# A transformer kernel with two blocks: fetched expert rows moved to a later stage, and the first projections and two stage seams put in another order

## What is computed

```
xn = rmsnorm(h, norm1_w); proj = xn @ w_in            # first block
h = h + (g_d * (o_d @ w_branch_diff) + g_c * (o_c @ w_branch_chunk)) @ w_out
h = h + peer(rmsnorm(h, norm2_w), ...)                # experts
h = rmsnorm(h, final_norm_w)
h = concat(meta, h)                                   # second block, 528 tokens
for layer in (0, 1):                                  # 0: gated deltanet, 1: mLSTM
    h = h + mixer(rms_norm(h, attn_norm[layer]))
    f = relu(rms_norm(h, ffn_norm[layer]) @ ff_up)
    h = h + (f * f) @ ff_down
```

## Time and profile before

| | us |
|---|---|
| median of 3 runs | 3837.25 |
| lowest, highest | 3832.71, 3839.84 |
| the profiled execution, its own time | 3834.99 |
| its span in the trace | 3833.2 |
| PE busy in the span | 3612.8 (94%) |
| DVE busy | 2439.8 (64%) |
| ACT busy | 1604.8 (42%) |
| POOL busy | 726.8 (19%) |

### The profile page before, as it was taken

One profiled execution on the slowest core, in us unless ns is written; L12 is line 12 of the kernel. 1 busy time (PEld: TensorE's weight loads), 2 busy tenths in 40 slices (PEclk: granted clock), 3 DMA queues, 4 the chain that ended last, 5 costly groups with the idle time before them and its releaser, 6 DMA issues.

```text
span 3833.2 us, 60211 instructions
## 1 busy us (share of the span) xinstructions
PE 3612.8 (94%) x24325; PEld 3370.2 (88%) x24325; DVE 2439.8 (64%) x4877; ACT 1604.8 (42%) x3002; POOL 726.8 (19%) x618
## 2 busy tenths in 40 slices
PE   7999999999999999999899999999899999979999
PEld 5777878999898999999788888888799989979999
DVE  5665349997768888888676676666643433455242
ACT  4555324336863333333454444443432335454141
POOL 0000004775443333332121111110000011010000
PEclk9999999999999999999899999999999999989999
DMA  3122224777889898989253332221222212212221
GB/s 122 61 67 69 91 83 138 239 240 245 257 293 338 318 345 319 331 318 338 71 82 55 61 63 57 60 61 31 73 88 94 94 34 67 67 56 83 94 94 61
DMA packets 208149, 542.30 MB, mean 141 GB/s; under 512 B 18665, under 2 KB 92905, under 8 KB 207873
## 3 DMA queue, kind: packets, MB, share of 16 engines
q1 hardware_dynamic: 99792, 341.22, 26.3%
q0 software_dynamic: 42048, 150.49, 13.7%
q10 hardware_dynamic: 66032, 46.75, 3.9%
HBM read 492.14 MB, written 46.25 MB: 140 GB/s over the span
## 4 chain that ended last, share of the span: by engine, by line
PE 65%; DVE 13%; ACT 12%; issue 5%; DMA 4%; ACTq 1%; POOL 1%; PEldq 0%; DVEq 0%; PEld 0%; POOLq 0%
PE bank L106 64%; ACT wh L127 4%; DVE wl L133 3%; DMA raw<-in_v 2%; ACT gb L127 2%; DVE acc L143 2%; ACT oh L127 1%; DVE row L179 1%; ACTq L187 1%; PE bank L109 1%; ACT L121 1%; DVE aal L133 1%; ACT rt L127 1%; DVE fs L133 1%; ACT L127 1%
## 5 line engine op out<-in xcount | busy, mean ns | idle before, releaser
L106 PE MATMUL bank<-Xh,wh 128*128 128x256 f32 (+3 forms) x3680 | 1222.4, 332 | 41.6 <-DVE Xl L133 21.0
L106 PE MATMUL bank<-Xl,wh 128*128 128x256 f32 (+3 forms) x3680 | 1156.8, 314 | 0.0
L106 PE MATMUL bank<-Xh,wl 128*128 128x256 f32 (+3 forms) x3680 | 1156.0, 314 | 0.0
L127 ACT ACTIVATE wh<-raw 128x1024 fp32r<-128x1024 f32 (+1 forms) x632 | 587.8, 954 | 678.0 <-PE bank L106 560.4
L133 DVE TENSOR_TENSOR wl<-raw,wh 128x1024 fp32r<-128x1024 f32 (+1 forms) x539 | 573.6, 1083 | 428.9 <-ACT wh L127 423.5
L106 PEld LDWEIGHTS bank<-Xh,wh 128*128 128x128 f32 x3680 | 705.6, 192 | 109.8 <-issue 65.6
L106 PEld LDWEIGHTS bank<-Xh,wl 128*128 128x128 f32 x3680 | 703.9, 191 | 20.6
L106 PEld LDWEIGHTS bank<-Xl,wh 128*128 128x128 f32 x3680 | 706.4, 192 | 17.6 <-issue 0.3
L133 DVE TENSOR_TENSOR H<-H,bank 128x256 f32<-128x256 f32 (+3 forms) x394 | 183.9, 469 | 325.8 <-PE bank L106 324.0
L106 PE MATMUL bank<-aah,wh 128*128 128x384 f32 x1024 | 350.9, 343 | 17.3 <-DVE wl L133 12.1
L106 PE MATMUL bank<-aal,wh 128*128 128x384 f32 x1024 | 347.9, 340 | 0.0
(11 more groups left out here) (340 smaller groups left out, 5940.0 us busy)
## 6 DMA issues: line engine op xcount, KB each, us to landing
raw<-in_u SPq DMA_DIRECT2D x128, 512.0 KB
raw<-in_v SPq DMA_DIRECT2D x128, 512.0 KB
raw<-in_up SPq DMA_DIRECT2D x64, 512.0 KB, 3.9
raw<-in_down SPq DMA_DIRECT2D x64, 512.0 KB, 3.3
scratch<-gb ACTq DMA_DIRECT2D x12, 2048.0 KB, 12.6
gj<-scratch SPq DMA_DIRECT2D x32, 768.0 KB
raw<-in_w_gdn SPq DMA_DIRECT2D x48, 512.0 KB
raw<-in_w_att SPq DMA_DIRECT2D x36, 512.0 KB
```

The source lines that it names most:

```text
L106: return Issued(self, self.q and self.q.matmul(out, l, r, start=start, stop=stop), 1)
L127: return Issued(self, self.q.activation(out, in_, func, **kw), 1)
```

## The change

ROWS_FIRST goes from 56 to 32, so that no row step lies beside the one-hots and 224 are left for the second part, with other numbers in some(n) and ONEHOT at 1.9. The first three projections take x times the norm weight, split on ACT and DVE into ODH and ODL (buffers that attention fills later), without the inverse root; DVE multiplies that in as it evicts (first_copy); each projection is a group of its own, and the norm blocks, which later projections read, lie between. DVE's first wait is for cols alone. Ahead of each feed-forward stage the last two sums of squares go behind the first two of the first three groups, and the norm of the second half behind the first three groups' relu2. The core of the diff (of the two raw_x the first is DVE's, the second ACT's; constants is DVE's):

```diff
-ONEHOT = 2.3
+ONEHOT = 1.9
-ROWS_FIRST = 56
+ROWS_FIRST = 32
 ...
         def first_unit():
+            x1 = [(16, 528)]
+            sums_begin("norm1", x1, PA)
+            for k in range(8):
+                if k < ADDED:
+                    sums_part("norm1", 16, k, f"x_in{k // 2}", 0)
+                do("raw_x", k)
+                if k == 3:
+                    prepare(1)
+            prepare(1)
+            def project(kind):
+                n = slab("w_att", kind)
+                (QT, KT, VT)[kind].take(0)
+                g = ATT_G[0, kind] = group(PD, by_slab(n), of(ODH, ODL), 512, lambda k: (("rxl", k),))
+                dense_now(g)
+                return n, g
+            def evict(kind, n, g):
+                do("first_copy", kind)
+                given_back(g, "qkv0", 0, kind)
+                done_with(n, g)
+            first = project(0)
+            for k in range(ADDED, 8):
+                sums_part("norm1", 16, k, f"x_in{k // 2}", 0)
+            prepare(1)
+            sums_end("norm1", x1)
+            second = project(1)
+            evict(0, *first)
+            for k in range(4):
+                norm_block("norm1", 16, 528, k)
+            third = project(2)
+            evict(1, *second)
+            for k in range(4, 6):
+                norm_block("norm1", 16, 528, k)
+            VF.take(0)
+            evict(2, *third)
+            for k in range(6, 8):
+                norm_block("norm1", 16, 528, k)
+            do("constants_in")
+            do("lam")
 ...
-                merge((itertools.chain(back(m, 1, 4), back(m + 1, 0, 0)), 32), (weighted(d), 44), (some(4), 4))
+                merge((itertools.chain(back(m, 1, 4), back(m + 1, 0, 0)), 32), (weighted(d), 44), (some(5), 5))
 ...
-                    side = some(6 + n % 2)
+                    side = some(8)
                     for j in (2 * (n % 2), 2 * (n % 2) + 1):
                         neurons(g, (j,))
                         next(side, None)
-                    merge((steps, 16), (side, 4 + n % 2))
+                    merge((steps, 16), (side, 6))
 ...
-        def ffn(layer):
+        def ffn(layer, behind):
-            sums_end(f"ffn{layer}", halves[1:])
-            xf = normed(f"ffn{layer}", halves, done=(halves[0][0],))
+            def xf(a, k):
+                return (("xl", f"ffn{layer}", a, k),)
 ...
-                        dense_together(gs)
+                        first = (half, fbs[0], a) == (0, 0, halves[0][0])
+                        if first:
+                            dense_together(gs[:2])
+                            for x in behind:
+                                sums_part(*x)
+                            sums_end(f"ffn{layer}", halves[1:])
+                            dense_now(gs[2])
+                        else:
+                            dense_together(gs)
 ...
+                        if first:
+                            for k in range(8):
+                                norm_block(f"ffn{layer}", *halves[1], k)
 ...
             def constants():
-                dv.wait_ge("const", 2)
-                dv.wait_ge("ones", 1)
+                dv.wait_ge("cols", 0)
+            def raw_x(k):
+                dv.wait_ge("rxh", k)
+                dv.stt(ODL[:, k, :], H[:, k, 16:528], col("norm1", k), ODH[:, k, :].bitcast(F32), ALU.mult,
+                       ALU.subtract).then_inc("rxl", k)
+            def first_copy(kind):
+                g = ATT_G[0, kind]
+                b = clear(dv, (QT, KT, VF)[kind], 0)
+                dv.wait_ge("rinv", "norm1", 16)
+                dv.wait_ge("dense", g)
+                dv.tt(b, PS[PD.at["g", g]], RT.at["norm1", 16][:, 0:512], ALU.mult).then_inc("qkv0", 0, kind)
 ...
+            def raw_x(k):
+                if k == 0:
+                    ac.wait_ge("cols", 0)
+                if k >= ADDED:
+                    ac.wait_ge(f"x_in{k // 2}", 0)
+                ac.act(ODH[:, k, :], H[:, k, 16:528], ACT.Copy, scale=col("norm1", k)).then_inc("rxh", k)
```

More of the change, by code:

```diff
@@ L607, in build, with xn @@
         do("lam_load")
[L608 to L615, removed]
+        def xn(a, k):
+            return (("xl", "norm1", a, k),)
         QT = Ring([alloc("qt", 512) for _ in range(2)])
@@ L631, in first_unit @@
         def first_unit():
[L632 to L635, removed]
-            VF.take(0)
[L637 to L642, removed]
+            x1 = [(16, 528)]
[30 more added lines that the diff above has]
+                norm_block("norm1", 16, 528, k)
+            VF.take(0)
+            evict(2, *third)
[3 more added lines that the diff above has]
+            do("lam")
         def proj_att(u):
@@ L1320, in last_outputs @@
                         prepare(1)
-            for x in behind:
-                sums_part(key, *x)
             for s in ws:
                 done_with(s, g)
+            return [(key, *x) for x in behind]
         GW = []
@@ L1708, in build @@
         ROOM[0] = room_at, more_room(("up0", "down0"), 1, 3, (("so", 7, 8), ("vnm", 7, 8), ("sn", 7, 7, 1)), room_at)
-        last_outputs(0, [("gdn_out", 14), ("gdn_out", 15)], OX.at[7], "ogl", XQ7, last_outs())
-        ffn(0)
+        behind = last_outputs(0, [("gdn_out", 14), ("gdn_out", 15)], OX.at[7], "ogl", XQ7, last_outs())
+        ffn(0, behind)
         fence()
@@ L1963, in build @@
         ROOM[1] = room_at, more_room(("up1", "down1"), 1, 3, (("mo", 3, 8), ("msn", 3, 7), ("mnum", 3, 2)), room_at)
-        last_outputs(1, [("ml_out", 6), ("ml_out", 7)], OX1.at[3], "mogl", XQ3, last_third())
-        ffn(1)
+        behind = last_outputs(1, [("ml_out", 6), ("ml_out", 7)], OX1.at[3], "mogl", XQ3, last_third())
+        ffn(1, behind)
         do("store")
@@ L1998, in constants, with constants_in @@
             def constants():
-                pe.wait_ge("const", 2)
                 pe.wait_ge("ones", 1)
+            def constants_in():
+                pe.wait_ge("const", 1)
             def dense(g, k):
@@ L2323, in pe_program @@
             program(pe, dict(
-                fence=fence, constants=constants, dense=dense, rms_sum=rms_sum, rms_total=rms_total, rms_part=rms_part, meta_sum=meta_sum, att_vt=att_vt, scores=scores, transp=transp,
+                fence=fence, constants=constants, constants_in=constants_in, dense=dense, rms_sum=rms_sum, rms_total=rms_total, rms_part=rms_part, meta_sum=meta_sum, att_vt=att_vt, scores=scores, transp=transp,
                 values=values, key_scores=key_scores, first_scores=first_scores, weights_out=weights_out, x_rows=x_rows, row_sums=row_sums,
@@ L2913, in dv_program @@
             program(dv, dict(
-                fence=fence, constants=constants, split=split, norm=norm, rms_part=rms_part, meta_reduce=meta_reduce, meta_scale=meta_scale, meta_low=meta_low, both_inv=both_inv, resid=resid, lam=lam, scores=scores,
+                fence=fence, constants=constants, constants_in=constants_in, raw_x=raw_x, first_copy=first_copy, split=split, norm=norm, rms_part=rms_part, meta_reduce=meta_reduce, meta_scale=meta_scale, meta_low=meta_low, both_inv=both_inv, resid=resid, lam=lam, scores=scores,
                 weigh=weigh, att_split=att_split, gated=gated, merge=merge, top16=top16, first_top=first_top, pairs=pairs, picked=picked,
@@ L2933, in constants @@
             def constants():
-                ac.dma(CB_, X["cols"][:, :]).then_inc("const", 0)
-                ac.dma(ROWP[0:16, 0:4], X["rows"][:, :]).then_inc("const", 1)
-                ac.dma(CST, X["cst"].rearrange("p (a b) -> p a b", a=9)).then_inc("const", 2)
+                ac.dma(CB_, X["cols"][:, :]).then_inc("cols", 0)
+                ac.dma(ROWP[0:16, 0:4], X["rows"][:, :]).then_inc("const", 0)
+                ac.dma(CST, X["cst"].rearrange("p (a b) -> p a b", a=9)).then_inc("const", 1)
                 ac.dma(H[:, :, 0:16], X["meta"].rearrange("p (k t) -> p k t", k=8)).then_inc("meta", 0)
@@ L3377, in ac_program @@
             program(ac, dict(
[L3378 removed]
+                fence=fence, constants=constants, split=split, rms_sum=rms_sum, rms_squares=rms_squares, rms_part=rms_part, rms_inv=rms_inv, norm=norm, raw_x=raw_x, x_load=x_load, meta_square=meta_square, meta_inv=meta_inv, meta_high=meta_high, both_inv=both_inv, lam=lam, att_copy=att_copy,
                 att_vt=att_vt, exps=exps, transp=transp, att_out=att_out, att_split=att_split, gate=gate,
```

9 lines of the change are left out of this document (5 added, 4 removed).

## The result

| | before | after |
|---|---|---|
| median of 5 runs, us | 3838.46 | 3858.34 |
| lowest, highest | 3832.71, 3839.84 | 3856.56, 3861.34 |
| span of the profiled execution | 3833.2 | 3855.8 |

The account below looks back on a forecast made before the run. PE, busy 94%, was taken as the bound, so only its waits could give time back. Terms -4 - 7 - 4 + 7 - 2.5 = -10.5 put the profiled execution near 3824.5 us, the median near 3827; range 3811 to 3845.

Parts of the forecast that it names:

- Start: Start of the kernel: first scores reach DVE at 47.8 instead of 52.74; -4 us, bounds 0 and -12.8.
- Seams: Both feed-forward seams: PE's waits shorten and the second half ends earlier; -3.5 us each, -7 together, bounds 0 and -13.3.
- two of the three first groups end near 2739.1, inside today's wait: First seam: these groups run while PE now waits 6.93 us for the last squares.
- What is late next is this second norm: Seams: the second half's norm, behind three relu2, replaces the squares as the late part; a wait of 3 to 4 us.
- One-hots: One-hot stage and choice of experts: -18.5 us, held spills seven to four, against +14.3 in the choice; -4 net.
- Second part: Weighted and neuron rounds: 24 more row steps and gathers cost +7 us in all, bounds 0 and +37.
- I let a third of it through: Neuron rounds: six steps add 7.5 us of DVE each; a third of that reaches the time, +7 in all.
- hidden by 4 us of slack: Weighted rounds: one more row step adds 1.25 us to DVE's 30.5 of 34.5, at no cost.
- slower: Rival, 0.12: DVE's in-order list bounds the second part, from some 95% share in neuron stretches; 30 instead of 7, 3850 us.
- Last round: Last round of the second part: without row steps DVE no longer delays the transpositions; -2.5 us, bounds 0 and -4.
- Transfers: Rival, 0.09: DMA at 356 GB/s bounds the neuron rounds; three pay 21 us instead of 7, 3841.
- the 358 GB/s: Rule against the forecast: HBM bound per core, neuron rounds not under 74.6 us, some 20 us added instead of 7.

Follow-up runs that it names:

- e4_rows_flat: The kernel after with its additional row steps in the weighted rounds alone (10 each; 26 in a neuron round, 6 in the last): 3846.15 us, 1.0026.
- e8_filled: The kernel after with the same row steps, one standing between DVE's af and the next slab's low part in neuron rounds: 3836.78 us, 0.9995.

## Why the prediction was wrong

- **Start** (-4): the mechanism and its times came out, within 1 us for most. The row quoted for the slow clock has 3.75 us for four matmuls, so it doesn't give the 0.43 of the working, but in after the first projection's matmuls do stand 0.43 apart. The end of the kernel doesn't show the gain (between -2.3 and +4.6); the sum took it as kept to the end.
- **Seams** (-7): they cost 4.6 where they stand, and 2.9 of that came back between them. The failed step is "two of the three first groups end near 2739.1, inside today's wait". I asked only when their input is ready. The groups need three banks, which the last three additions to H hold; the matmuls then ran at a clock of 0.51, close to 1.2 GHz, and the sums came behind them. "What is late next is this second norm" was right, and worth 4.9 a seam.
- **One-hots** (-4 net): -22.4 and +14.1, so -8. The price in the choice and the count of held spills were right; the holds also got shorter, which I had not allowed for.
- **Second part** (+7): +27.7. The failed step is "I let a third of it through". All of it went through in the neuron rounds, 1.2 us a step (20.9 for the 18 that `e4_rows_flat` took out), and 0.2 a step in the weighted ones, where "hidden by 4 us of slack" was nearly right. I took DVE's idle 16% for slack, though much of it was a wait inside a loop. The rival "slower" had the list in order, but "It decides from where DVE's share in a neuron stretch passes some 95%" was wrong: it decided at 84%, and the other order ran the neuron parts at 92%, 19.4 us shorter. Even so the rival's thought that DVE's load counts was right in part: in that order the added steps still cost 15.0.
- **Last round** (-2.5): -0.4. The 2.2 us ahead of the transposition stayed; six row steps fewer in front of it changed nothing, and both traces name DVE's addition to H as what ended it.
- **Transfers:** without the gathers the time does not change beyond its interval. As for the 358 GB/s: the first stretch of `e8_filled` averages just 358, but nine of its slices of 2.75 us in a row hold 399 to 410, so it is no ceiling:

```profile
GB/s 270 295 176 395 384 365 338 268 273 365 398 383 392 328 207 343 358 366 408 409 399 405 410 410 408 408 404 279 201 401 391 416 399 401 407 407 392 322 348 383
```

  The Trainium skill's page "HBM Reference", section "Specifications (TRN2)", says a core that streams alone measures well above its share, about 425; this trace agrees, with slices of up to 416.

## What to carry to other kernels

An engine's idle share is slack only if its idle time stands where added work can go. Look at what ends each idle time: if it is an engine that waits for this one in turn, added work is paid whole, unless it is put into that wait itself, behind the instruction that the other engine waits for. Even there it isn't free: here that took the price from 25.6 us down to 15.0. So compare with the kernel before in the same better order, not only in its old one. And ask of a group that is started early not only for its input but for its PSUM banks.

## What I had not expected

- One DVE instruction with two inputs in SBUF took 3.38 us instead of 1.28 beside a POOL tensor_tensor, which took 2.92.
- A spill's issue behind a 2 MB g_out is held for less when no row gathers lie beside it: at most 4.4 us in the kernels with 24 row steps there, at most 2.3 in those with none, with the same 4.8 us between the two issues. Within each of the eight traces with 24 row steps, the two spills held least (1.5 to 2.0 us) have no gather issued in the 5.9 us ahead of the g_out, and the other five (2.7 to 4.4 us) have one 0.7 to 1.4 us ahead of it. That is seen in every trace, but its cause was not tried.
- Two profiles of one kernel can be 5 us apart in the middle and 1.5 at the end.
- The order in which ACT makes aah and wh, the other side of the loop, was not tried.
